# The prompt's gathered rows padded to 128 partitions in the expert stage of a two-sequence encoder layer

## The reference

```python
def expert_choice_ffn(x, w_router, w_gate, w_up, w_down):
    ...
    cap = CAPACITY_FACTOR * T // N_EXPERTS
    h = x.reshape(T, d)
    aff = jax.nn.softmax((h @ w_router).astype(jnp.float32), axis=-1)
    gate_vals, tok_idx = lax.top_k(aff.T, cap)
    xg = h[tok_idx]
    hid = jax.nn.silu(jnp.einsum('ecd,edf->ecf', xg, w_gate)) * jnp.einsum('ecd,edf->ecf', xg, w_up)
    out = jnp.einsum('ecf,efd->ecd', hid, w_down) * gate_vals[..., None].astype(x.dtype)
    y = jnp.zeros_like(h).at[tok_idx.reshape(-1)].add(out.reshape(-1, d))
    return y.reshape(b, s, d)
```

## Time and profile before

| | us |
|---|---|
| median of 3 runs | 3694.23 |
| lowest and highest | 3691.44, 3696.48 |
| the profiled execution | 3689.45 |
| its span in the trace | 3687.6 |
| TensorE matmuls busy | 3435.1 (93%) |
| VectorE, ScalarE, GpSimd busy | 2331.2, 1893.5, 409.3 |

### The profile page before, as it was taken

One profiled execution on the slowest core, in us unless ns is written; L12 is line 12 of the kernel. 1 busy time (PEld: TensorE's weight loads), 2 busy tenths in 40 slices (PEclk: granted clock), 3 DMA queues, 4 the chain that ended last, 5 costly groups with the idle time before them and its releaser, 6 DMA issues. The chain is left out here.

```text
span 3687.6 us, 61850 instructions
## 1 busy us (share of the span) xinstructions
PE 3435.1 (93%) x20358; PEld 3124.9 (85%) x20358; DVE 2331.2 (63%) x3830; ACT 1893.5 (51%) x3320; POOL 409.3 (11%) x373
## 2 busy tenths in 40 slices
PE   8999699788939999999999999999999999999993
PEld 6888699566829899998989999898998989899992
DVE  6421067687657676666757667675776767667674
ACT  3222167342316565555656556565565656556564
POOL 0011064333200000000000000000000000000003
PEclk9999889898969999999999999999999999999997
DMA  4222353133327777767777777777777777677775
GB/s 165 77 66 74 85 143 99 43 110 110 128 75 233 236 230 236 237 213 232 235 222 233 234 235 221 235 235 218 236 230 221 232 239 235 217 234 224 237 234 184
DMA packets 240063, 699.41 MB, mean 190 GB/s; under 512 B 52960, under 2 KB 68608, under 8 KB 239520
## 3 DMA queue, kind: packets, MB, share of 16 engines
q1 hardware_dynamic: 225920, 648.13, 54.9%
q0 software_dynamic: 13056, 45.29, 4.8%
q10 hardware_dynamic: 864, 3.15, 0.2%
HBM read 642.89 MB, written 57.77 MB: 190 GB/s over the span
## 5 line engine op out<-in xcount | busy, mean ns | idle before, releaser
L1847 PE MATMUL moe_gu<-moe_xgT,moe_whi 128*128 128x384 f32 x5632 | 1634.4, 364 | 7.6 <-issue 3.6
L1979 DVE TENSOR_TENSOR moe_wlo<-moe_raw,moe_whi 128x1024 fp32r<-128x1024 f32 x1056 | 1290.3, 1223 | 484.0 <-ACT moe_whi L1933 483.4
L1848 PE MATMUL moe_gu<-moe_xgT,moe_wlo 128*128 128x192 f32 x5632 | 1414.1, 251 | 0.0
L1933 ACT CAST moe_whi<-moe_raw 128x1024 fp32r<-128x1024 f32 x1056 | 1106.1, 1048 | 443.9 <-PE moe_dnp L1863 389.1
L1848 PEld LDWEIGHTS moe_gu<-moe_xgT,moe_wlo 128*128 128x128 f32 x5632 | 1083.7, 192 | 0.4
L1847 PEld LDWEIGHTS moe_gu<-moe_xgT,moe_whi 128*128 128x128 f32 x5632 | 1065.2, 189 | 13.0 <-issue 4.9
L1940 ACT COPY moe_part<-moe_gu 128x384 f32<-128x384 f32 x352 | 168.7, 479 | 459.2 <-PE moe_gu L1848 459.2
L1985 DVE TENSOR_TENSOR moe_guv<-moe_gu,moe_part 128x384 f32<-128x384 f32 x352 | 196.3, 558 | 292.5 <-ACT moe_part L1940 292.5
L1812 POOL DMA_INDIRECT tmp_acc<-moe_og_s,moe_srow_s x16 | 25.7, 1608 | 2286.4 <-ACT moe_og_s L1965 2286.4
L1859 PE MATMUL moe_dns<-moe_whi,moe_hid 128*128 128x512 f32 x704 | 275.9, 392 | 0.0
L1862 PE MATMUL moe_dnp<-moe_whi,moe_hid 128*128 128x512 f32 x704 | 275.6, 392 | 0.0
(11 more groups left out here) (275 smaller groups left out, 4128.6 us busy)
## 6 DMA issues: line engine op xcount, KB each, us to landing
moe_raw<-in_w_ffn SPq DMA_DIRECT2D x1056, 512.0 KB, 4.1
prj_wraw<-in_w_in SPq DMA_DIRECT2D x12, 1024.0 KB, 5.4
att_raw<-tmp_qkT SPq DMA_DIRECT2D x32, 384.0 KB, 7.0
prj_share<-in_xT SPq DMA_DIRECT2D x6, 1024.0 KB, 10.4
tmp_qkT<-prj_share POOLq DMA_DIRECT2D x24, 256.0 KB, 2.7
ssd_xb<-tmp_xbc SPq DMA_DIRECT2D x12, 512.0 KB, 3.9
mix_rows<-in_x SPq DMA_DIRECT2D x12, 512.0 KB, 5.2
tmp_h<-mix_rows SPq DMA_DIRECT2D x12, 512.0 KB, 2.6
```

What stands on the lines that cost most here:

```text
L1847: pe.matmul(out[:, a, 0:2 * CAP], whi[c][:, j, :], x, start=(j == 0), stop=False)
L1848: mm = pe.matmul(out[:, a, 0:CAP], wlo[c][:, j, :], x[:, 0:CAP], start=False, stop=(j == KD - 1))
L1933: act.copy(whi[c][:], raw[c][:]).then_inc(hi_done, 1)
L1979: dve.tensor_tensor(wlo[c][:], raw[c][:], whi[c][:].bitcast(F32), ALU.subtract).then_inc(lo_done, 1)
```

## The change

`xg_p` gets 128 partitions. Its upper half is set to zero once, by VectorE at the start of the stage, and TensorE waits for that once (`xg_pad`). The gather writes the lower 64 partitions as before. The transpose of the prompt's block is now 128 by 128 with the whole identity, and writes 128 columns, of which the upper 64 are zeros that nobody reads. To make room, a fill's two column blocks now stand 256 columns apart in their bank instead of 192, and the two readers take 192 of each 256.

```diff
-        xg = [m.sb("xg_s", [NS, D]), m.sb("xg_p", [NP_, D])]
+        xg = [m.sb("xg_s", [NS, D]), m.sb("xg_p", [P, D])]
...
-        tr = [dns[:, b, :] for b in range(2)]
+        tr = [dns[:, b, :].rearrange("p (j c) -> p j c", j=2) for b in range(2)]
...
+        xg_pad = m.sem("xg_pad")
...
-                    pool.indirect_dma_start(xg[i][:], None, dram["h"], bass.IndirectOffsetOnAxis(ap=grow[i][:], axis=0)).then_inc(xg_in, 16)
+                    pool.indirect_dma_start(xg[i][0:CAPS[1 - i], :], None, dram["h"], bass.IndirectOffsetOnAxis(ap=grow[i][:], axis=0)).then_inc(xg_in, 16)
...
-                    pe.transpose(tr[b % 2][:, CAP * j:CAP * j + NS], xg[0][:, P * k:P * k + P], ident[:])
-                    mm = pe.transpose(tr[b % 2][:, CAP * j + NS:CAP * j + CAP], xg[1][:, P * k:P * k + P], ident[0:NP_, 0:NP_])
+                    pe.transpose(tr[b % 2][:, j, 0:P], xg[0][:, P * k:P * k + P], ident[:])
+                    mm = pe.transpose(tr[b % 2][:, j, P:2 * P], xg[1][:, P * k:P * k + P], ident[:])
...
             pe.wait_ge(const_in, 32)
+            pe.wait_ge(xg_pad, 1)
             pe.wait_ge(xg_in, 32)
...
-                act.copy(xgT[q][:, 2 * b:2 * b + 2, 0:CAP], tr[b % 2][:, 0:2 * CAP].rearrange("p (j c) -> p j c", j=2)).then_inc(tok_hi, 1)
+                act.copy(xgT[q][:, 2 * b:2 * b + 2, 0:CAP], tr[b % 2][:, :, 0:CAP]).then_inc(tok_hi, 1)
...
+            dve.memset(xg[1][NP_:, :], 0.0).then_inc(xg_pad, 1)
...
-                dve.tensor_tensor(xgT[q][:, 2 * b:2 * b + 2, CAP:2 * CAP], tr[b % 2][:, 0:2 * CAP].rearrange("p (j c) -> p j c", j=2),
+                dve.tensor_tensor(xgT[q][:, 2 * b:2 * b + 2, CAP:2 * CAP], tr[b % 2][:, :, 0:CAP],
```

## The result

| | before | changed |
|---|---|---|
| median, us | 3695.36 | 3654.64 |
| lowest and highest | 3691.44, 3698.33 | 3646.29, 3657.02 |
| profiled execution; its span | 3689.45; 3687.6 | 3656.00; 3654.2 |

The ratio is 0.9888 with an interval of 0.9874 to 0.9902: about 41 us less, where 29 were forecast. The median lies 0.4 us under the low end of the range. The direction and the price of a group were right; the saving was 12 us larger than the sum. One execution of e12 took 4810.6 us at a mean granted clock of 0.64, where the others have 0.95 to 0.97, and is left out of its median and ratio.

A forecast was written before the change was run, and what follows sets the result against it. It took TensorE's own queue as the bound and summed 24.8 us (25 full-clock groups), 3.0 (five at 1.2 GHz) and 1.4 (opening) to 29.2 us saved: 3665 us against the 3694.23 median, range 3655 to 3676.

The forecast's parts named there:

- TensorE's queue is the bound: Expert stage: waits are next to nothing in 2500 us, so time taken out of TensorE's queue comes off the total.
- The price of the new transposes: Groups of eight at full clock: 0.11 us per transpose, 0.88 a group instead of 1.87, gaining 0.99.
- The opening: First 16 transposes, at 1.2 GHz with a copy and subtraction chain: gate/up starts 1.4 us earlier.
- The memset and the readers: VectorE's one memset fits in idle time and the gapped reads take no longer: 0 us.
- The token chain, rival (a): Second group of each expert: subtractions come late, 14.8 us given back, 3680 us; chance 0.05. Main forecast: 0.29 us cover holds.
- Why the pairs were dear: Transpose pairs at 0.46 us: the 64-row height of every second transpose was taken as what differs from line 1344.
- The five groups at 1.2 GHz: Groups behind waits for ScalarE's output rows: 1.1 us shorter each, about 0.6 kept, 3.0 us in all.
- Rival (e): Slow-clock stretches around six waits come out differently: 3658 to 3668 us; chance 0.86 together with the main forecast.
- rival (d): Dense transpose blocks lower the granted clock in each of 30 groups: 21 us more, 3715 us; chance 0.02.

The follow-up runs named there:

- e12: A repeat of e6, the changed kernel with its fills behind gate/up chunks 1 and 3: 3625.6 us, ratio 0.9822 to the kernel before.
- e8: The kernel before, run again with no edit: ratio 0.9997.
- e2: The kernel before with only the new PSUM places (column blocks 256 apart), prompt transposes still 64 by 64, no memset: ratio 1.0012.
- e3: The kernel before, each fill turning both sample blocks first and then both prompt blocks, without padding: ratio 0.9945.
- e7: The kernel before, each group turning four sample blocks and then four 64-high prompt blocks, without padding: 3657.9 us, ratio 0.9904.
- e1: The changed kernel, run again with no edit: ratio 0.9899 to the kernel before.
- e4: The changed kernel with each fill's transposes issued twice, same values to the same place: 3679.1 us, ratio 0.9976 to the kernel before.
- e10: The same kernel as e4, run a second time: 3682.0 us, ratio 0.9965 to the kernel before.
- e9: The kernel before with each fill's transposes issued twice, heights still alternating: 3775.4 us, ratio 1.0218.
- e5: The kernel before with the fills behind gate/up chunks 1 and 3 in place of 0 and 1: 3664.6 us, ratio 0.9922.
- e6: The changed kernel with the fills behind gate/up chunks 1 and 3 in place of 0 and 1: 3627.5 us, ratio 0.9831 to the kernel before.
- e11: e7's order without padding, with the fills behind gate/up chunks 1 and 3 as in e6: 3632.2 us, ratio 0.9833 to the kernel before.

## Why the prediction was wrong

What the profiles show of each kernel's groups, clock and stage:

| | group, us | waits with a stretch at 1.2 GHz | these stretches, us | stage, us |
|---|---|---|---|---|
| before | 1.78 | 6 of 6 | 34.1 | 2523.6 |
| e8, before again | 1.78 | 6 of 6 | 37.5 | 2526.7 |
| e2, only the places in PSUM | 1.78 | 6 of 6 | 30.7 | 2525.1 |
| e3, two and two | 1.21 | 4 of 6 | 20.5 | 2499.7 |
| e7, four and four | 0.91 | 4 of 6 | 17.1 | 2493.6 |
| changed | 0.79 | 4 of 6 | 13.7 | 2486.4 |
| e1, changed again | 0.79 | 2 of 6 | 10.2 | 2481.7 |
| e4, dense doubled | 1.66 | 0 of 6 | 0 | 2508.7 |
| e10, dense doubled again | 1.66 | 3 of 6 | 10.2 | 2512.6 |
| e9, alternating doubled | 3.62 | 6 of 6 | 51.2 (88.7 with those at other groups) | 2611.6 |
| e5, before without the wait | 1.78 | no wait | 0 | 2494.6 |
| e6, changed without it | 0.79 | no wait | 0 | 2461.9 |
| e12, e6 again | 0.79 | no wait | 0 | 2459.2 |
| e11, e7 without it | 0.91 | no wait | 0 | 2465.1 |

- **TensorE's queue is the bound: right.** What a group lost came off the time, 1.02 us for 1.02 (e5 against e6 and e12).
- **The price of the new transposes: right.** 0.11 us from start to start, as in line 1344; the group gains 1.87 - 0.85 = 1.02 where 0.99 was taken.
- **The opening: right.** From 6.80 to 5.38 us (1108.12 to the first gate/up matmul at 1113.49), 1.4 less. TensorE waits once for a subtraction between the fills, 0.3 us.
- **The memset and the readers: right.** The memset takes 0.91 us, from 1095.83, and the gathered rows land 11 us after it.
- **The token chain, rival (a): right that it holds**, with 0.27 us against the 0.29 computed.
- **Why the pairs were dear: named by halves.** The prediction saw the height as the likely cause. e7 shows that it's the alternation of heights; among themselves the 64-high ones are cheaper still.
- **The five groups at 1.2 GHz: wrong. This is the step that failed.** It said "I take it that the shorter transposes don't end it sooner" and credited 5 x 0.6 = 3.0 us. Behind the dense groups it ended sooner, or didn't come. From the start of such a group to the start of the next, the kernel before takes 53.3 us in the six places (e8 54.9, and e2 52.0), where six undisturbed ones take 6 x 6.45 = 38.7; the changed kernel takes 38.9 (e1 37.3) where they take 6 x 5.44 = 32.6. The loss to the clock is 15.4 us on average of before and e8, and 5.5 on average of changed and e1. So these places gave 10 us beyond the plain price of their groups, while the sum had 2 less than it for five of them.
- **Rival (e) had the right place and the wrong cause.** It held the stretches for chance, centred on no change, and gave 7 us at most to the good side. That the group behind the wait could matter, and that a stretch could be missing altogether, was not considered, though rival (d) had suspected the dense block of the reverse. That the median came to within 0.4 us of the range is owed to (e), whose 7 us stood in its low end for a reason that wasn't the right one.

The new sum: 30 x 1.02 + 1.4 + 9.9 for the clock = 41.9, less 1.7 us for waits that were longer on average in the two profiles of the changed kernel (TensorE's idle time in the stage: 23.9 against 22.2 us), and less 0.9 for the stretch in the first expert, which one of the two has. That is 39.3; the stage shows 41.1 (mean of before and e8, 2525.2, less mean of changed and e1, 2484.1), the medians 41 and 38.

**What stays open.** Why one wait is followed by a stretch and the next isn't: behind the six waits e4 had none and e10, the same kernel, three. Nor is it shown what in an alternating group brings the stretches, the wider spacing of the starts or the change of height as such; the orders of e3 and e7 lie between (4 of 6 waits each), but one profile of each is too few to rank them. Nor are height and width told apart: a transpose streams a square identity, so both change together, and this wasn't tried. With e7's 0.06 us between 64-high neighbours the question hardly matters here.

## What to carry to other kernels

Don't let transposes of different heights alternate on TensorE: sort them by height, or pad the low ones where that is free. Here each change of height cost about 0.15 us, more than a transpose does among its own kind (0.11 or 0.06). And when a part of the program stands behind a wait, look at the granted clock beside it: here what stood behind the wait changed how much of the next microseconds ran at 1.2 GHz, so an edit there can be worth more or less than its own duration. Better still, take the wait away: moving the fills a chunk or two later saved 23.5 us more in the stage of the changed kernel (2484.1 to 2460.6, each the mean of two profiles).

## What the runs showed of the hardware

- At full clock, fp32 transposes start 0.11 us apart if both are 128 by 128, 0.06 if both are 64 by 64, and 0.15 to 0.26 where the height changes (e3, e7 and the earlier trace rows); at 1.2 GHz the dense ones start 0.21 apart.
- The granted clock fell to 0.50 at the end of a group of alternating transposes of 3.6 us, with no idle time on TensorE before it (e9, at 1453.60). It stayed at 1.00 through a wait of 2.4 us and the dense group of 1.66 us behind it (e4, at 1595.79). Behind a wait of 1.2 us with an alternating group of 1.78 us it fell (before, at 2222.86).
- The stages that weren't touched vary by 12 us from one execution to another (1159.9 to 1172.4), which is more than most of the effects that were looked for.
